# Opening of a two-block model kernel: q, k and v products of the first head between the modulation units

## What is computed

```python
ada = silu(c) @ w_ada[l] + b_ada[l]
shift, scale, gate = split(ada, 3)
h = rmsnorm(x, norm_g[l]) * (1 + scale) + shift
mq, mk, mv, mo, mz, mi, mf, rq, rk, rv, rz = split_cols(h @ w_in[l])
qk = silu(causal_dwconv(concat(mq, mk)))        # 4 taps
cell = mlstm_chunkwise(q, k, mv, mi + b_i, mf + b_f)   # 4 heads of 256
y_m = sigmoid(mo) * head_layernorm(cell) * silu(mz)
y_r = head_layernorm(retention(rotary(rq), rotary(rk), rv)) * silu(rz)
x = x + gate * (concat(y_m, y_r) @ w_out[l])
```

## Time and profile before

| | |
|---|---|
| median of 3 runs | 2087.67 us (2086.46 to 2089.18) |
| profiled execution | 2089.77 us, of which span 2087.9 us |
| TensorE busy, share of the span | 2047.5 us, 98% |
| VectorE busy | 1752.3 us, 84% |
| ScalarE busy | 1322.0 us, 63% |
| o of head 0 starts | t = 64.15 |
| bytes moved by DMA | 597.37 MB, 286 GB/s in the mean |

### The profile page before, as it was taken

The page is one execution under the profiler, slowest core; times in us unless marked ns, Lnnn a source line. Parts: engine busy times, 40 slices in busy tenths (PEclk is TensorE's granted clock), DMA queues, the critical chain, the costliest instruction groups (busy, mean ns, idle before and its releaser), DMA issues.

```text
span 2087.9 us, 33390 instructions
## 1 busy us (share of the span) xinstructions
PE 2047.5 (98%) x13347; PEld 1829.9 (88%) x13347; DVE 1752.3 (84%) x2155; ACT 1322.0 (63%) x1267; POOL 31.1 (1%) x60
## 2 busy tenths in 40 slices
PE   7999999999999999999999999999999999999998
PEld 5999999999999799999878888888888888888887
DVE  3898976888759778888768889898898989899897
ACT  3655555665645663435667777776777777777774
POOL 3000000000000000000000000000000000000000
PEclk8999999999999999999999999999999999999999
DMA  9787865766656569987548999999999999999995
GB/s 295 254 265 230 250 210 173 226 214 195 219 179 218 170 213 311 313 325 230 165 165 297 365 356 355 376 365 349 359 357 377 360 351 362 368 368 355 358 357 189
DMA packets 358817, 597.37 MB, mean 286 GB/s; under 512 B 10985, under 2 KB 204025, under 8 KB 358665
## 3 DMA queue, kind: packets, MB, share of 16 engines
q1 hardware_dynamic: 355248, 588.72, 82.0%
q0 software_dynamic: 2752, 5.86, 1.1%
q10 hardware_dynamic: 664, 0.66, 0.1%
HBM read 591.80 MB, written 4.22 MB: 285 GB/s over the span
## 4 chain that ended last, share of the span: by engine, by line
PE 78%; DVE 12%; ACT 3%; DMA 3%; issue 3%; SPq 1%; POOL 0%; DVEq 0%; POOLq 0%; ACTq 0%
PE ps L1729 10%; PE ps L1731 10%; PE ps L1730 10%; PE ps L1760 5%; PE ps L1759 5%; PE ps L1758 5%; PE ps L1203 3%; PE ps L1260 3%; PE ps L1204 3%; PE ps L1205 3%; PE ps L1261 3%; PE ps L1262 3%; DVE wlo L1827 3%; DVE acc L1883 3%; ACT whi L774 2%
## 5 line engine op out<-in xcount | busy, mean ns | idle before, releaser
L1827 DVE TENSOR_TENSOR wlo<-raw,whi 128x2048 fp32r<-128x2048 f32 x485 | 1108.7, 2289 | 190.2 <-ACT whi L774 187.6
L774 ACT CAST whi<-raw 128x2048 fp32r<-128x2048 f32 x485 | 926.4, 1911 | 350.4 <-PE ps L1731 123.3
L1203 PE MATMUL ps<-hhi,whi 128*128 128x256 f32 x1360 | 387.9, 285 | 0.0
L1204 PE MATMUL ps<-hlo,whi 128*128 128x256 f32 x1360 | 380.4, 280 | 0.0
L1205 PE MATMUL ps<-hhi,wlo 128*128 128x256 f32 x1360 | 380.2, 280 | 0.0
L1729 PE MATMUL ps<-whi,xghi 128*128 128x512 f32 x896 | 355.2, 396 | 0.7 <-DVE wlo L1827 0.7
L1731 PE MATMUL ps<-wlo,xghi 128*128 128x512 f32 x896 | 349.8, 390 | 0.0
L1730 PE MATMUL ps<-whi,xglo 128*128 128x512 f32 x896 | 349.1, 390 | 0.0
L1203 PEld LDWEIGHTS ps<-hhi,whi 128*128 128x128 f32 x1360 | 256.5, 189 | 3.9 <-issue 3.6
L1204 PEld LDWEIGHTS ps<-hlo,whi 128*128 128x128 f32 x1360 | 256.5, 189 | 0.2
L1205 PEld LDWEIGHTS ps<-hhi,wlo 128*128 128x128 f32 x1360 | 256.4, 189 | 0.0
(11 more groups left out here) (415 smaller groups left out, 2990.2 us busy)
## 6 DMA issues: line engine op xcount, KB each, us to landing
raw<-in_moe_w_gate_dram SPq DMA_DIRECT2D x112, 1024.0 KB, 6.0
raw<-in_moe_w_up_dram SPq DMA_DIRECT2D x112, 1024.0 KB, 6.2
raw<-in_moe_w_down_dram SPq DMA_DIRECT2D x112, 1024.0 KB, 5.2
raw<-in_w_in_dram SPq DMA_DIRECT2D x92, 1024.0 KB, 5.6
raw<-in_w_ada_dram SPq DMA_DIRECT2D x69, 1024.0 KB, 7.9
raw<-in_w_out_dram SPq DMA_DIRECT2D x24, 1024.0 KB, 5.2
raw<-in_ffn_w_gate_dram SPq DMA_DIRECT2D x11, 1024.0 KB, 8.8
raw<-in_ffn_w_up_dram SPq DMA_DIRECT2D x11, 1024.0 KB, 8.7
```

The source lines that it names most:

```text
L774: nc.scalar.copy(whi[:, u.hl, :], raw[:, u.raw, :]).then_inc(hi_ready, 1)
L1203: mm(ps2[u.bank][:, j], whi[:, u.hl, w], hhi[:, k], start=k == 0, stop=False)
L1204: mm(ps2[u.bank][:, j], whi[:, u.hl, w], hlo[:, k], start=False, stop=False)
L1827: V.tensor_tensor(wlo[:, u.hl, :], raw[:, u.raw, :], whi[:, u.hl, :].bitcast(F32), ALU.subtract).then_inc(raw_free, 1)
```

## The change

- SyncE: c, c_2 and ident move from SyncE's queue to the head of ScalarE's. The weight units of q, k and v are loaded between the first eight modulation units: q behind the second, k and v behind the fourth.
- ScalarE: q's whi is made before the first pair of h, k's before and v's behind the second pair.
- VectorE: q's low part is made before the first modulation, k's and v's behind the second.
- TensorE: `opening_products(i, parts)` multiplies q, k and v by those parts k of the contraction that exist, between `ada_start` and `turn_rows`; `turn_rows(0)` comes directly behind the norm; three matmuls of `keep_busy` stand behind `turn_rows(1)`. v goes to bank 4 instead of bank 0. Only its parts 6 and 7 are left for head 0.
- Head 0 on TensorE: o and z come as `low_last_products` (the 32 matmuls with whi first, then the 16 with wlo, which alone wait for the low part), z and the gate columns before the broadcast and the scores; rq comes before the values; the head's mean goes into the middle of rk.
- Head 0 on VectorE: the convolution of q first, then the gates' takeover, o's low part, the convolution of k, the gate sums, z's low part.
- All other heads keep their order.

```diff
--- before.py
+++ after.py
...
@@ -541,9 +541,6 @@
 
         @block.sync
         def _(sp):
-            for i, v in enumerate((c, c_2)):
-                sp.dma_start(crow[KD * i:KD * (i + 1), :], v[0].rearrange("(k p) -> k p", p=P)).then_inc(c_in, 16)
-            sp.dma_start(ident, consts[:, C_ID:C_ID + P]).then_inc(ident_in, 16)
             sp.dma_start(xtok[:], x[0].rearrange("(t p) d -> p t d", p=P)).then_inc(x_in, 16)
 
             def load(u, src, k):
@@ -578,15 +575,15 @@
                                  w_ada[0].rearrange("(k p) n -> p k n", p=P)[:, :, 256 * a[3]:256 * a[3] + 256]).then_inc(spare_in[i], 16)
                 else:
                     ada_load(*a)
-                if a[0].n == FIRST_UNIT_AT:
-                    load(Unit(S_B1), w_in[0].rearrange("(k p) n -> p k n", p=P)[:, :, 0:HD], KD)
+                for i in UNITS_BEHIND.get(a[0].n, ()):
+                    load(Unit(S_B1 + i), w_in[0].rearrange("(k p) n -> p k n", p=P)[:, :, i * D_MLSTM:i * D_MLSTM + HD], KD)
             for l in range(L):
                 wl = w_in[l].rearrange("(k p) n -> p k n", p=P)
                 u0 = Unit(S_B1 + l * UNIT_L1)
                 for j in range(H * HEAD_UNITS):
                     part, hd = j % HEAD_UNITS, j // HEAD_UNITS
                     col = part * D_MLSTM if part < 5 else RET_COL + (part - 5) * D_RET
-                    if l or j:
+                    if l or j >= FIRST_UNITS:
                         load(u0.plus(j), wl[:, :, col + hd * HD:col + hd * HD + HD], KD)
                     if l == 0 and j == 4:
...
+                    take_rows(1)
+                    high(Unit(S_B1 + 1))
+                    norm_pair(0, 1)
+                    high(Unit(S_B1 + 2))
+                    for p in (2, 3):
+                        take_rows(p)
                         norm_pair(0, p)
-                        if p == 1:
-                            high(Unit(S_B1))
-                    high(Unit(S_B1 + 1))
                 gates_high(l)
                 for h_no in range(H):
                     hd = Head(l, h_no)
                     q, k, v, o, z, rq, rk, rv, rz = hd.units
-                    high(q.plus(LOOK))
+                    if hd.n:
+                        high(q.plus(LOOK))
                     act.wait_ge(unit_done, q.done())
                     if hd.n:
...
                 for j in range(2):
+                    if j and between:
+                        between()
                     for k in range(KD):
                         w = slice(256 * k + P * j, 256 * k + P * j + P)
                         mm(ps2[u.bank][:, j], whi[:, u.hl, w], hhi[:, k], start=k == 0, stop=False)
                         mm(ps2[u.bank][:, j], whi[:, u.hl, w], hlo[:, k], start=False, stop=False)
                         last = mm(ps2[u.bank][:, j], wlo[:, u.hl, w], hhi[:, k], start=False, stop=k == KD - 1)
+                last.then_inc(unit_done, 1)
+
+            def opening_products(i, of):
+
+                u = Unit(S_B1 + i)
+                if of[0] == 0:
+                    pe.wait_ge(raw_free, u.free())
+                for k in of:
+                    pe.wait_ge(hlo_ready, k + 1)
+                    for j in range(2):
+                        flags = dict(stop=False, skip_group_check=True)
+                        if i < 2:
+                            w, o = slice(256 * k + P * j, 256 * k + P * j + P), ps2[u.bank][:, j]
+                            mm(o, whi[:, u.hl, w], hhi[:, k], start=k == j == 0, **flags)
+                            mm(o, whi[:, u.hl, w], hlo[:, k], start=False, **flags)
+                            last = mm(o, wlo[:, u.hl, w], hhi[:, k], start=False, stop=k == KD - 1, skip_group_check=True)
+                        else:
+                            w, s, o = slice(256 * k, 256 * k + 256), slice(P * j, P * j + P), ps2[FIRST_V_BANK][:, j]
+                            mm(o, hhi[:, k, s], whi[:, u.hl, w], start=k == j == 0, **flags)
+                            mm(o, hlo[:, k, s], whi[:, u.hl, w], start=False, **flags)
+                            last = mm(o, hhi[:, k, s], wlo[:, u.hl, w], start=False, stop=k == KD - 1, skip_group_check=True)
+                if of[-1] == KD - 1:
+                    last.then_inc(unit_done, 1)
+
+            def low_last_products(u, between=None):
+
+                pe.wait_ge(hi_ready, u.count())
+                for j in range(2):
+                    for k in range(KD):
+                        w, o = slice(256 * k + P * j, 256 * k + P * j + P), ps2[u.bank][:, j]
+                        mm(o, whi[:, u.hl, w], hhi[:, k], start=k == j == 0, stop=False, skip_group_check=True)
+                        mm(o, whi[:, u.hl, w], hlo[:, k], start=False, stop=False, skip_group_check=True)
+                if between:
+                    between()
+                pe.wait_ge(raw_free, u.free())
+                for j in range(2):
+                    for k in range(KD):
+                        w, o = slice(256 * k + P * j, 256 * k + P * j + P), ps2[u.bank][:, j]
+                        last = mm(o, wlo[:, u.hl, w], hhi[:, k], start=False, stop=k == KD - 1, skip_group_check=True)
                 last.then_inc(unit_done, 1)
 
...
@@ -1338,14 +1371,31 @@
             pe.wait_ge(memset_done, 2)
             pe.wait_ge(cfirst_ready, 1)
             pe.wait_ge(x_ready, 4)
-            for a in ADA_AT_START:
-                n = a[0].n
-                ada_start(a[0])
-                if n == 1:
-                    norm(0)
-                if n >= 2 and n % 2 == 0:
-                    turn_rows(n // 2 - 1)
+            starts = [a[0] for a in ADA_AT_START]
+            ada_start(starts[0])
+            ada_start(starts[1])
+            norm(0)
+            turn_rows(0)
+            ada_start(starts[2])
+            ada_start(starts[3])
+            opening_products(0, (0, 1))
+            turn_rows(1)
+            keep_busy(OPENING_WAIT, 7)
+            opening_products(0, (2, 3))
+            opening_products(1, (0, 1, 2, 3))
+            ada_start(starts[4])
+            ada_start(starts[5])
+            opening_products(2, (0, 1))
+            turn_rows(2)
+            opening_products(2, (2, 3))
+            ada_start(starts[6])
+            opening_products(0, (4, 5))
+            ada_start(starts[7])
+            opening_products(1, (4, 5))
             turn_rows(3)
+            opening_products(2, (4, 5))
+            opening_products(0, (6, 7))
+            opening_products(1, (6, 7))
 
...
@@ -1417,19 +1466,30 @@
                             mm(sums, ghi[:, d], hlo[:, d], start=False, stop=False)
                             last = mm(sums, glo[:, d], hhi[:, d], start=False, stop=d == KD - 1)
                         last.then_inc(gates_done, 1)
-                    pe.wait_ge(taken_s, hd.count(7, 1))
-                    token_products(v)
-                    ada_after(2)
-                    if h_no == 0:
+
+                    def turn_gates():
                         pe.wait_ge(a_ready, l + 1)
                         for t in range(2):
                             last = mm(ps[5][:, t * H:(t + 1) * H], g_a[:, t * P:(t + 1) * P], ident[0:H, 0:H], start=True, stop=True)
                         last.then_inc(a_turned, 1)
+
+                    if hd.n:
+                        pe.wait_ge(taken_s, hd.count(7, 1))
+                        token_products(v)
                     else:
+                        opening_products(2, (6, 7))
+                    ada_after(2)
+                    if l and not h_no:
+                        turn_gates()
+                    elif h_no:
                         pe.wait_ge(spread_gates, l + 1)
                         broadcast_gates(h_no)
                     pe.wait_ge(taken_s, hd.count(7, 2))
-                    products(o)
+                    if hd.n:
+                        products(o)
+                    else:
+                        low_last_products(o)
+                        low_last_products(z, turn_gates)
                     ada_after(3)
                     if h_no == 0:
                         pe.wait_ge(spread_gates, l + 1)
@@ -1437,24 +1497,34 @@
                         broadcast_gates(h_no)
                     pe.wait_ge(act_done, hd.count(1, 1))
                     scores(qk)
-                    pe.wait_ge(taken_s, hd.count(7, 3))
-                    products(z)
-                    ada_after(4)
+                    if hd.n:
+                        pe.wait_ge(taken_s, hd.count(7, 3))
+                        products(z)
+                        ada_after(4)
+                    else:
+                        pe.wait_ge(taken_s, hd.count(7, 4))
+                        products(rq)
                     pe.wait_ge(sT_ready, hd.count(2, 1))
                     pe.wait_ge(v_ready, hd.count(2, 1))
                     values(ps2[4], True)
-                    pe.wait_ge(taken_s, hd.count(7, 4))
-                    products(rq)
+                    if hd.n:
```

(64 more changed lines are left out.)

39 lines of the change are left out of this document (15 added, 24 removed).

## The result

The changed kernel takes 2095.81 us (median of 7 executions, 2092.79 to 2096.85), the kernel before 2087.73 (7 executions, 2084.83 to 2089.87): ratio 1.0038, 95% interval 1.0028 to 1.0048. It is 8.1 us slower; 5.9 had been forecast. The profiled execution took 2096.79 us, 1.0 above the median, with a span of 2094.9 us.

A forecast was written before the change was run, and what follows sets the result against it. VectorE was taken to carry the end up to t = 169, TensorE from 172. Gates 2.5, Silu 1.1 and values 2.3 summed to +5.9 us on 2087.67, giving 2093.6 us (chance 0.40), range 2085.5 to 2098.0.

The forecast's parts named there:

- Direction and mechanism: Whole kernel: slower, because VectorE, not TensorE, carries the end up to 169; slower by more than 0.2% given 0.53.
- rival A: Up to 169: TensorE's stream of products carries the end, so its lead stands, faster at 2080.2 to 2085.3; chance 0.16.
- B: Opening: the clock holds at full, gates at 57.6, total +3.0 us, 2090.7; chance 0.21.
- D: Opening and head 0 cancel within 1 us, so the change does nothing; chance 0.06.
- T: Start of the first modulation unit: 13.0 instead of 14.08, from the DMA queue move; bounds 0 and 1.2 us gain.
- The opening: Up to head 0's gates: TensorE idles 4.1 us, then half clock; gates done at 60.5 against 58.0, 2.5 us late.
- Silu: Head 0, gates done to Silu: 10.85 us instead of 9.77, with gate exponential and table load uncovered, +1.1 us.
- The values: Head 0: values stand behind rq, at Silu + 12.75 against 10.46, delaying VectorE's next split by 2.3 us.
- The sum at the split of 82.93: VectorE's split behind head 0's values: gates 2.5, Silu 1.1, values 2.3 make +5.9 us, at about 88.8.
- The gap before rq: Head 0, TensorE: a new idle of about 3 us; 2.2 us more if the clock falls, left out of the sum.
- the one in head 1: TensorE before head 1's values: idle of about 3 us; 2.2 us more if the clock falls, left out of the sum.
- rival C: The clock also falls in TensorE's gaps, adding 2.2 or 4.4 us: 2095.8 or 2098.0; chance 0.17.

The follow-up runs named there:

- e9: Kernel before with head 0's new order alone, opening and DMA queue as before; 4.1 us above the kernel before, interval 1.0007 to 1.0025.
- e1: Changed kernel plus four unused matmuls in each of two TensorE gaps (before rq, before head 1's values); +6.8 us against the kernel before.
- e10: Changed kernel with ident alone back at the head of SP's queue, ahead of x; 2094.33 us.
- e6: Changed kernel with head 0's old order, q converted before the norm's root, ident heading SP's queue; 2084.41 us, 3.3 below the kernel before.
- e3: Changed kernel with head 0's gate sums put back ahead of k's half of the convolution on VectorE; +4.6 us against the kernel before.

## Why the prediction was right, point by point

**Direction and mechanism: right.** In 89 to 131 VectorE is busy 41.23 of 42 us in the changed kernel, and its one listed wait there is the end of the one at 89.35; TensorE, at 38.55, now has the slack:

```profile
89.00:131.00 42.00, 38.55 (x314) 37.67 (x313) 41.23 (x83) 24.29 (x31) 1.59 (x3) 1.00 0.81 247
```

o starts at 60.8, 3.3 us earlier than before, and of that lead nothing is left at the second head. Up to 169 VectorE isn't unbroken, though: behind the late values of head 1 it waits 1.04, 1.29 and 0.60 us (151.59, 153.31, 157.45) for ScalarE and TensorE, where it waited 0.34 before (144.97). There the path runs through TensorE. e9 speaks against the stream of products (rival A of the prediction): a loss of 4.1 us without work added. e1 does so at its mark, not in its median. Rivals B and D fall with the granted clock of 0.50 and the result.

**T: mis-sized, 13.85 for 13.0.** The step that failed is ident's. I had taken a value between an ident that isn't held up and one that takes as long as the parameter load; it was the second. In the eight traces with ident on ScalarE's queue it is waited for until 6.9 to 8.6 us, and T is 13.6 to 15.3, mean 14.2; with ident at the head of SP's it comes by 3.5. The parameter loads came at 12.7, where I had 12.3. With ident back in front of x they came at 13.02 and 12.14, and T was 13.39 (e10) and 12.76 (e6), on either side of the 13.0.

**The opening: +2.5 forecast, +1.5 in the first pair of traces, +2.2 over all.** Six traces with the changed opening, q in its place and keep_busy have gates at 59.4 to 60.5 (mean 59.9), three of the old opening with the old queues at 57.3 to 58.1 (mean 57.7). The idle of 4.1 us was 4.52, with half clock behind it, as forecast; the clock was back at 36.5 instead of 38.3, and modulation 3 came at 51.69 instead of 52.75 although T was late. No wait of TensorE for a DMA is left behind T, as forecast.

**Silu: +1.1 forecast, +0.9 measured** (10.63 from gates to Silu, 9.72 before). The terms that the prediction lists add to 10.65, not to the 10.85 written there, so each of them held. The table load of 68.92 takes 1.28 and Silu follows at 70.22, so the drain of about 1.38 us that the Trainium skill (ScalarE: Activation LUTs, "What ACT_TABLE_LOAD costs") adds to a load isn't there either where the load stands on the path. e3 shows what it costs that the sums stand behind the convolution.

**The values: +2.3 forecast; the mechanism was right.** Silu to values is 14.55 against 10.46, +4.1, of which 1.6 is the fall inside rq (e10) and 2.5 the order.

**The sum at the split of 82.93: 88.8 forecast, 89.35 measured.** That close an agreement is partly luck: Silu came at 70.22, 1.1 before the forecast 71.3, and from there to the values it took 14.55 instead of 12.75, 1.8 more, 1.6 of it a fall of the clock that the sum had left out. The gap before rq was 2.66 (3 forecast), the one in head 1 2.86 (3). Whether the clock would fall in them I had left out of the sum and made rival C, 2095.8 or 2098.0. In the changed kernel's trace it fell in both: 1.6 us in rq, and 2 in head 1, where the split behind the values moved from 6.4 to 8.3 us late. From the split behind head 0's values to that behind head 1's it is 63.96 in the two traces with a fall between (changed and e10), and 62.0 to 62.2 in the other eleven. Against the second trace of before that makes 2.3 (gates) + 0.9 + 4.1 + 2 = 9.3 of the 9.7 at the mark. Without the two falls the mark would be some 6.1 late (9.7 less 1.6 and 2), near the 5.9 forecast. So the 2.2 us between forecast and result are rival C's term, in part: not every execution has both falls (e10 has one of the two). That the median lies at C's lower figure, 2095.8, says no more than that.

**The pair from page to row.** The Trainium skill (DMA: Bandwidth & Descriptors, "Queues, rings and completion order") says that a DMA engine takes turns between queues packet by packet. By that ident, a load of 64 KB issued at 1.70, should not have waited behind x; it landed 5.4 us after its issue, 1.3 behind x (issued at 0.73, landed 5.1 later). Here the measurement decides against a full gain from a second queue; what held ident up is not shown.

**Still open:** what decides whether an idle of a given length costs a fall (below), and how often each fall comes in the executions that were not profiled, so how much of the 8.1 us is steady. No run separates keep_busy's gain from the scatter of the opening.

## What to carry to other kernels

A product moved into a gap brings its conversions with it: ask where these stand in the queues of the engines that feed the critical step. Here q's two conversions stood ahead of the first modulation and cost 5.3 us, and moving them ahead of the norm's root, with ident back on SP's queue, turned the opening's loss of 3.5 us into a gain of 3.3. A lead of one engine is worth nothing while another hands over the work: it turns into gaps, and gaps can turn into half clock. And compare an early mark over two traces of the kernel before, since one trace can be off by 2.4 us at 250, and look in each trace for falls ahead of the mark before calling a difference the edit's.
